# Opening norm in two halves, with the latent projection issued slice by slice behind the first half

## The reference

```python
u = rms_norm(h, norm_mix[l])            # h = x, 1024 x 1024
proj = u @ w_in[l]
z_rwkv, c_q, c_kv, k_rope, gate_a, gate_b = _split(proj, IN_SIZES)
# c_q, c_kv, k_rope: 256 + 128 + 32 = 416 latent columns
ang = positions.astype(jnp.float32)[..., None] * inv_freq
cos, sin = jnp.cos(ang), jnp.sin(ang)
...                                     # y_b: latent attention over c_q, c_kv, k_rope
...                                     # y_a: RWKV-7 scan over z_rwkv
h = h + merged @ w_out[l]
h = h + jnp.square(jax.nn.relu(rms_norm(h, norm_ffn[l]) @ w_ff_up[l])) @ w_ff_down[l]
return rms_norm(h, norm_final)
```

## Time and profile before

| | |
|---|---|
| Time before, median of 3 runs | 1726.64 us (1726.24 to 1730.62) |
| Profiled execution, its own time | 1740.58 us |
| Span of the profiled execution | 1738.9 us |
| Mean granted TensorE clock | 0.976 of 2.4 GHz |
| PE busy | 1648.5 us, 95% of the span |
| DVE busy | 898.5 us, 52% |
| ACT busy | 553.1 us, 32% |
| POOL busy | 95.0 us, 5% |

### The profile page before, as it was taken

The page is one execution under the profiler, slowest core; times in us unless marked ns, Lnnn a source line. Parts: engine busy times, 40 slices in busy tenths (PEclk is TensorE's granted clock), DMA queues, the critical chain, the costliest instruction groups (busy, mean ns, idle before and its releaser), DMA issues.

```text
span 1738.9 us, 26191 instructions
## 1 busy us (share of the span) xinstructions
PE 1648.5 (95%) x10627; PEld 1315.4 (76%) x10627; DVE 898.5 (52%) x1490; ACT 553.1 (32%) x979; POOL 95.0 (5%) x175
## 2 busy tenths in 40 slices
PE   3999998899999998999989979999999999999996
PEld 2985665677878887885777868888888888888885
DVE  5357875477763832567762154444444444444437
ACT  6433454244342113444221143222222222222222
POOL 0110000000010010356000000000000000000000
PEclk9996999999999999999999989999999999999998
DMA  5020001522223354003444002111111111111102
GB/s 185 1 58 1 2 1 38 133 73 70 83 70 119 97 140 154 3 4 117 145 142 160 1 25 85 49 49 48 48 48 48 48 48 48 48 48 48 37 0 109
DMA packets 122566, 114.40 MB, mean 66 GB/s; under 512 B 24303, under 2 KB 106348, under 8 KB 121836
## 3 DMA queue, kind: packets, MB, share of 16 engines
q1 hardware_dynamic: 122368, 113.10, 21.1%
q10 hardware_dynamic: 108, 0.03, 0.0%
HBM read 90.14 MB, written 21.00 MB: 64 GB/s over the span
## 4 chain that ended last, share of the span: by engine, by line
PE 87%; DVE 7%; DMA 2%; issue 1%; ACT 1%; SPq 1%; DVEq 0%; ACTq 0%
PE bank L2283 20%; PE bank L2296 19%; PE bank L1917 18%; PE bank L2259 5%; PE bank L2217 4%; PE bank L1852 3%; PE bank L1760 2%; PE bank L1881 2%; PE bank L1865 2%; PE bank L1826 2%; DMA posi<-in_positions 1%; PE bank L2018 1%; PE bank L2127 1%; PE bank L2121 1%; PE bank L1790 1%
## 5 line engine op out<-in xcount | busy, mean ns | idle before, releaser
L1705 DVE TENSOR_TENSOR hacc<-hacc,bank 128x512 f32<-128x512 f32 x240 | 163.5, 687 | 134.6 <-PE bank L2296 134.6
L2283 PE MATMUL bank<-hT_hi,up_hi 128*128 128x512 f32 x512 | 199.8, 390 | 3.2 <-DVE up_lo L1682 3.2
L2296 PE MATMUL bank<-dn_hi,f_hi 128*128 128x512 f32 x512 | 199.4, 389 | 1.4 <-DVE hacc L1727 1.4
L2283 PE MATMUL bank<-hT_hi,up_lo 128*128 128x512 f32 x512 | 199.9, 390 | 0.0
L2283 PE MATMUL bank<-hT_lo,up_hi 128*128 128x512 f32 x512 | 199.9, 390 | 0.0
L2296 PE MATMUL bank<-dn_hi,f_lo 128*128 128x512 f32 x512 | 199.2, 389 | 0.0
L2296 PE MATMUL bank<-dn_lo,f_hi 128*128 128x512 f32 x512 | 199.2, 389 | 0.0
L1917 PE MATMUL bank<-uT_hi,w_hi 128*128 128x512 f32 x480 | 191.8, 400 | 6.3 <-DVE w_lo L1369 6.3
L1158 ACT ACTIVATE frelu<-bank 128x512 f32<-128x512 f32 x64 | 38.3, 599 | 476.4 <-PE bank L2283 427.7
L1917 PE MATMUL bank<-uT_hi,w_lo 128*128 128x512 f32 x480 | 188.4, 393 | 0.0
L1917 PE MATMUL bank<-uT_lo,w_hi 128*128 128x512 f32 x480 | 188.4, 392 | 0.0
(11 more groups left out here) (343 smaller groups left out, 2741.1 us busy)
## 6 DMA issues: line engine op xcount, KB each, us to landing
up_raw<-in_w_ff_up SPq DMA_DIRECT2D x32, 512.0 KB, 5.4
dn_raw<-in_w_ff_down SPq DMA_DIRECT2D x16, 1024.0 KB, 5.0
w_raw<-in_w_in SPq DMA_DIRECT2D x30, 512.0 KB, 4.0
sgate<-gate_spill SPq DMA_DIRECT2D x16, 512.0 KB, 4.3
gate_spill<-zbuf SPq DMA_DIRECT2D x15, 512.0 KB, 2.7
xt<-in_x SPq DMA_DIRECT2D x8, 512.0 KB, 7.8
wout_raw<-in_w_out SPq DMA_DIRECT2D x8, 512.0 KB, 4.8
hacc<-in_x SPq DMA_DIRECT2D x8, 512.0 KB, 8.9
```

Source lines behind the costliest of these rows:

```text
L1705: nc.vector.tensor_tensor(hacc[:, n // 2, sl], hacc[:, n // 2, sl], ps[4 + n % 4][:], ALU.add).then_inc(s_da, 1)
L2283: ins = nc.tensor.matmul(ps[2 * q + h][:], st[:, q, k, :], mv_[:, k, sl], start=(k == 0 and m == 0), stop=(k == KD - 1 and m == 2))
L2296: ins = nc.tensor.matmul(ps[4 + n % 4][:], st[:, par, q, i * P:(i + 1) * P], mv_[:, par, q, sl], start=(q == 0 and m == 0), stop=(q == 1 a ...
```

## The change

- SyncE issues the positions first, ahead of x.
- ScalarE takes one root of a constant column ahead of its squares. The squares and the root are then done in two halves, four row tiles each.
- VectorE no longer waits for both of TensorE's small transposes before it works on the angles: the positions' transpose comes first and has a bank of its own (6). The mean, inverse root and scaling are done per half; the scaling of the second half stands behind the first half's low parts and `wc_lo`.
- ScalarE and VectorE alternate slice by slice: `uT_high(k)`, `wc_hi(k)`, and `uT_low(k)`, `wc_lo(k)`.
- TensorE transposes the first half (n 0 to 7), projects tile 0 slice by slice, each slice waiting for its `uT_lo` and `wc_lo`, then tile 1, transposes 8 to 11, tile 2, transposes 12 to 15, tile 3, tiles 4 and 5, the tables, tile 6, `transpose_c(0)`, tile 7.
- Sine and cosine move behind `take_c(0)`; the rounding of the up-projection weights behind `take_c(3)`; that of the first gate's weights behind `take_c(4)`.

The core of the diff:

```diff
             def _(sp):
+                sp.dma_start(posi[0:NT, :], a["positions"][0].rearrange("(i p) -> i p", p=P)).then_inc(s_pos, 16)
                 for i in range(NT):
                     sp.dma_start(xt[:, i, :], x_d[i]).then_inc(s_x[i], 16)
                 sp.dma_start(wc_raw[:], win[:, :, RWKV_COLS:RWKV_COLS + CC]).then_inc(s_wc, 16)
-                sp.dma_start(posi[0:NT, :], a["positions"][0].rearrange("(i p) -> i p", p=P)).then_inc(s_pos, 16)
...
+                act.wait_ge(s_const, 1)
+                nc.scalar.activation(small[:, 252:253], ident[:, 0:1], ACT.Sqrt)
+
+                for g in range(2):
+                    for i in range(4 * g, 4 * g + 4):
+                        act.wait_ge(s_x[i], 16)
+                        if i:
+                            act.wait_ge(s_ss, i)
+                        nc.scalar.activation(xjunk[:], xt[:, i, :], ACT.Square,
+                                             accum_out=small[:, i:i + 1]).then_inc(s_ss, 1)
+                    act.wait_ge(s_rt, 2 * g + 1)
+                    nc.scalar.activation(small[:, 16 + 4 * g:20 + 4 * g], small[:, 8 + 4 * g:12 + 4 * g], ACT.Sqrt).then_inc(s_rt, 1)
...
+                act.wait_ge(s_vcol, 1)
                 act.wait_ge(s_wc, 16)
                 for k in range(KD):
+                    uT_high(k)
                     nc.scalar.activation(wc_hi[:, k, :], wc_raw[:, k, :], ACT.Copy).then_inc(s_wch, 1)
...
                 take_c(0)
-                act.wait_ge(s_wc, 32)
-                nc.scalar.activation(ew_hi[:], ew_raw[:], ACT.Copy).then_inc(s_wch, 1)
+                act.wait_ge(s_sin, 1)
+                nc.scalar.activation(sinv[:], ang[:], ACT.Sin).then_inc(s_sin, 1)
+                nc.scalar.activation(cosv[:], ang[:], ACT.Sin, scale=0.5).then_inc(s_sin, 1)
                 take_c(1)
+                for n in range(KD, KD + 4):
+                    uT_high(n)
+                take_c(2)
+                for n in range(KD + 4, 2 * KD):
+                    uT_high(n)
+                take_c(3)
                 act.wait_ge(s_u, 32)
                 round_uq(0)
-                take_c(2)
                 round_uq(1)
...
-                for i in range(3, 5):
-                    take_c(i)
+                take_c(4)
+                act.wait_ge(s_wc, 32)
+                nc.scalar.activation(ew_hi[:], ew_raw[:], ACT.Copy).then_inc(s_wch, 1)
                 root_c(0)
...
+                mean_x(0)
+                dve.wait_ge(s_vcol, 1)
+                norm_x(0)
+                mean_x(1)
                 for k in range(KD):
+                    uT_low(k)
                     dve.wait_ge(s_wch, k + 1)
                     nc.vector.tensor_tensor(wc_lo[:, k, :], wc_raw[:, k, :], wc_hi[:, k, :].bitcast(F32),
                                             ALU.subtract).then_inc(s_wcl, 1)
+                norm_x(1)
 
                 dve.wait_ge(s_sin, 3)
...
+                for n in range(KD, 2 * KD):
+                    uT_low(n)
...
+                pe.wait_ge(s_posf, 1)
+                nc.tensor.transpose(ps[6][:, 0:NT], posr[0:NT, :], ident[0:NT, 0:NT]).then_inc(s_vt, 1)
                 pe.wait_ge(s_vec, 1 + 16 * len(VROWS))
                 nc.tensor.transpose(ps[7][:, 0:NV], vrow[0:NV, :], ident[0:NV, 0:NV]).then_inc(s_vt, 1)
...
                         if i == 0:
+                            pe.wait_ge(s_lo, k + 1)
                             pe.wait_ge(s_wcl, k + 1)
...
+                for n in range(KD):
+                    transpose_x(n)
+                project_c(0)
+                project_c(1)
+                for n in range(KD, KD + 4):
+                    transpose_x(n)
+                project_c(2)
+                for n in range(KD + 4, 2 * KD):
+                    transpose_x(n)
+                project_c(3)
                 pe.wait_ge(s_lo, 2 * KD)
-                for i in range(4):
-                    project_c(i)
+                project_c(4)
+                project_c(5)
                 tables()
-                for i in range(4, 7):
-                    project_c(i)
+                project_c(6)
                 transpose_c(0)
                 project_c(7)
```

## The result

The changed kernel took 1719.72 us (median of 10 runs, 1712.67 to 1727.84), beside 1730.29 for the kernel before on the same chips (10 runs, 1724.25 to 1737.85). The ratio is 0.9925, with a 95% interval of 0.990 to 0.995: 13.0 us less, 8.7 to 17.3 by the interval. Forecast were 12.4 us less, 1714.2, in 1706 to 1721. The medians lie 10.6 us apart, within the interval. The level is 5.5 us above 1714.2: 3.7 because the kernel before itself came out that much higher than in its first three runs, and 1.8 because the medians lie 10.6 apart where 12.4 was forecast.

The account below looks back on a forecast made before the run. The opening was held by positions, VectorE and norm, then TensorE; 31.9 + 34.8 + 3.5 + 0.3 put the first gate at 70.5 against 82.97, so 1726.6 - 12.4 = 1714.2 us, range 1706 to 1721.

Parts of the forecast that it names:

- The bound: Up to the first gate at 82.97: positions' transfer, VectorE and norm hold the opening, then TensorE is the chain, 42.4 us.
- Positions and norm: Opening: positions' work over by about 9 us under the squares, early root 0.2, first half normed at 16.3.
- The start of the slices: First uT_hi on ScalarE: starts at 19.3, released by the latent weights' transfer; bounds 18.0 and 24.3.
- The slices: Low parts on VectorE: 1.17 us per slice sets the pace, eighth wc_lo ends at 29.4.
- TensorE in the slices: Tile 0 of the latent projection: begins at 24.7 at half clock, full clock returns at 30.7, ends at 31.9.
- From tile 0 to the first gate: Rest of the opening: 34.8 us as before, plus 3.5 for moved transposes and 0.3 wait at transpose_c(0).
- (a): Start of the slices: wc_raw lands with the last transfers, 5.0 us later; gain 7.4, 1719.2 us; chance 0.08.
- (d): Latent projection: waits between slices bring half clock, which stays; seven tiles cost 26 us more, 1740; chance 0.04.
- (b): Attention's opening: half-clock stretch grows by a row block, 14 us more; 1728, no change; chance 0.08.
- (c): Attention's opening: half-clock stretch ends a row block sooner, 7.5 us less; 1707; chance 0.07.

Follow-up runs that it names:

- the runs in blocks: Changed kernel, all eight uT parts then all eight wc parts, no alternation: 1723.99 us; same with ScalarE's wait for latent weights behind the uT high parts: 1721.76 us.
- the weights ahead: Changed kernel, latent weights loaded between x's halves, second half's squares behind uT high parts, transpose groups 4 to 7 between tile 0's slices: ratio 0.9915.
- the run with both edits: Changed kernel with latent weights loaded between x's halves (and the reordering with it) plus identity transposes in attention's first three row blocks: ratio 0.9903.

## Why the prediction was right

**The bound.** Right. The opening was held by the positions, VectorE and the norm, and all else followed TensorE's list. Taking back the positions alone, or the halves and slices alone, took back part of the gain (first gate at 77.96 and 76.39), so both carry it. What was gained in the first 83 us is there at the first score (129.6 before, 116.1 after, 13.5).

**Positions and norm.** Right, with two parts that can be had separately (6.6 and 5.0). The early root, costed at 0.2, is paid under a wait and brings nothing.

**The start of the slices.** 19.3 forecast, 19.20 measured, released by the weights' load. An edit that no longer waits for the load got 1.0 us of it.

**The slices.** VectorE's pair of low parts at 1.17 forecast, 1.16 measured; last `wc_lo` to end at 29.4, ended at 29.30.

**TensorE in the slices.** This step held the only term that was off. Tile 0 started at 24.98 (24.7 forecast) and began at half clock, as taken. But full clock was back at 26.9, not 30.7. I had let the half clock begin with tile 0 and last the 6.0 us of the earlier trace rows. It began at about 23.5 (0.87 in 22 to 24), in the sparse groups, which is 1.2 of the 3.8 us; the other 2.6 are that it was shorter than in the kernel before, and why is not shown. Tile 0 ended at 30.6 instead of 31.9. That is 1.3 us in the gain's favour, and it is the whole difference between 70.5 and 69.45 but for two tenths the other way. Which end it takes is partly luck of the execution: with the same code tile 0 was taken out at 31.41 in two others, nearer the forecast. A slip in the working changed nothing: the four groups ahead of tile 0 were forecast from 20.7 to 24.7, which is 4.0 us and not 4.7.

**From tile 0 to the first gate.** 38.6 forecast, 38.8 measured. The added transposes cost 3.5, the wait at `transpose_c(0)` 0.3; nothing else waited. In one piece they would have cost 1.9 more.

**The rivals.** (a) did not come: `wc_raw` landed at 19.1. (d) did not come: half clock was over when tile 0's second slice was done. (b) and (c) are real in kind, but belong to neither kernel: with unchanged code, scores took 149.3 us in one run (transposes in one piece), 150.1 in another (transposes between slices), 153.0 in three and 155.1 to 156.8 in the rest. What differs is when full clock comes back: by 135 us in the first two, at 144 to 146 in the three, from 150 on in the rest. The second of those runs, and then the changed kernel:

```profile
130.00:135.00 5.00, 4.89 (x22) 2.42 (x20) 3.70 (x13) 1.70 (x6) 0.00 (x0) 0.52 0.00 0
135.00:140.00 5.00, 4.82 (x32) 2.49 (x30) 4.49 (x16) 1.70 (x6) 0.00 (x0) 1.00 0.00 0
```

```profile
145.00:150.00 5.00, 5.00 (x19) 2.67 (x18) 3.14 (x8) 1.34 (x4) 0.00 (x0) 0.52 0.00 0
```

The ten executions of the changed kernel differ with the clock too: those at a mean granted clock of 0.982 or more took 1712.7 to 1715.3 us, the one at 0.981 took 1719.1, and those at 0.978 or less 1719.1 to 1727.8. I gave (b) and (c) 0.15 together as effects of the change; the runs show them as scatter between executions, 7.5 us in this stage.

**Transposes, waits and the clock.** In the three runs that filled attention's waits with transposes of the identity the clock stayed at 1.00 over all scores, and in all eleven profiled executions without them it fell to half there. So transposes, put among the matmuls, helped to hold the full clock. The Trainium skill (TensorE: Matmul & The Clock Gate, Part 4: PE-mode transpose) says that they do not; these runs contradict it. The Trainium skill's rule that waits between groups of matmuls put the clock back (TensorE: Matmul & The Clock Gate, HAM oscillation) agrees with the runs in blocks (1.6 us) and with the weights ahead (3.0 us, once, since dense tiles followed), but in the run with both edits the same wait left the clock at full.

## What to carry to other kernels

When a norm over the whole input stands ahead of the first product, start the product on the half that is ready and put the other half's transposes, few at a time, between its row tiles; here they cost just their own 3.5 us. Look first for a small late transfer that the head of an engine's list waits for: moving 4 KB to the front of the queue gave 6.6 of the 13.5 us by itself. A pause of TensorE can cost twice, as the wait and as the half clock behind it: the same 2.8 us of wait cost 5.8 in one execution and 3.0 in another. For the same reason profile an edit more than once before a difference of 1 or 2 us is believed: a reordering that looked 4 us better came out 2.4 worse in one profile and 0.4 better in the next.

## What the runs showed of the hardware

The clock's column can say 1.00 where the pace says half. In the kernel before, the first 16 transposes ran at 0.21 us each under a granted 1.00, twice the 0.11 of the tables' transposes, and in the run with attention filled tile 0 ran at half pace until 28 us:

```profile
26.00:28.00 2.00, 2.00 (x8) 1.90 (x7) 2.00 (x4) 1.48 (x4) 0.00 (x0) 1.00 0.01 4
```

Eight matmuls in 2 us stand against 12 in the changed kernel's window from 28 to 30, at the same 1.00. The record seems to show nothing until full clock first comes in an execution; so in the opening the pace has to be read from start to start.

Work without use need not cost: with 106 transposes of the identity in TensorE's waits the scores took 149.9 us in all three profiles. Without them they took 149.3 to 156.8, in the mean of eleven 153.9. The gain of 5.7 us on the changed kernel's own profile is thus about 4 in the mean and none against the best; what the transposes took away is the scatter.

With identical code the clock fell in one execution and not in another (the slices, and the wait of 2.8 us), so a level read in one profile is not yet a property of the kernel.
